# Norm panels started ahead of their sums, a reordered state-space tail and one table for log and exp, in a three-block transformer kernel

## The reference, cut to what matters

```python
def reference(x, mem, positions, ...):          # x is 256 x 2048, fp32
    x = first_block(...)     # even layer: gate conv + state-space mixer + memory attention
                             # odd layer: latent attention (MLA) + memory attention; then rms_norm
    return second_block(x, ...)   # retention layer, then squared_relu_mlp, final rmsnorm

def rmsnorm(x, g):           # stands before every projection
    return x * rsqrt(mean(x * x) + 1e-6) * g

# state-space output of one of 4 groups (512 columns), before w_out:
y = (y_diag + y_off + xs * d) * silu(z)
y = y * rsqrt(mean(y * y) + 1e-6) * ssd_norm_w
# retention:
x = x + (head_norm(o) * silu(g)) @ ret_w_out     # 8 heads, 512 columns each
x = x + square(relu(rmsnorm(x) @ w_up)) @ w_down
```

## Time and profile before

| what | us |
|---|---|
| median of 3 timed runs | 2857.05 (2854.23 to 2864.59) |
| span of the profiled execution | 2861.9 |
| TensorE busy | 2769.8 |
| VectorE busy | 1954.6 |
| ScalarE busy | 1405.5 |
| mean granted TensorE clock over the span | 0.986 |

### The profile page before, as it was taken

The page is one execution under the profiler, slowest core; times in us unless marked ns, Lnnn a source line. Parts: engine busy times, 40 slices in busy tenths (PEclk is TensorE's granted clock), DMA queues, the critical chain, the costliest instruction groups (busy, mean ns, idle before and its releaser), DMA issues.

```text
span 2861.9 us, 46279 instructions
## 1 busy us (share of the span) xinstructions
PE 2769.8 (97%) x15792; PEld 2412.3 (84%) x15792; DVE 1954.6 (68%) x3079; ACT 1405.5 (49%) x2199; POOL 35.4 (1%) x56
## 2 busy tenths in 40 slices
PE   6999999999999899999999999999999999999998
PEld 5888888888888788888888888888888888888887
DVE  5566567787767777777666655666667677576775
ACT  5544245555554555556555534555554444444444
POOL 0000000000000001000000000000000000000000
PEclk9999899999999999999999999999999999999999
DMA  5555354444664334465454455454445555555553
GB/s 230 193 190 191 119 193 151 154 147 149 199 226 152 112 128 159 150 194 182 169 179 172 172 176 182 177 179 171 152 166 188 191 189 191 191 191 190 187 188 110
DMA packets 76338, 495.57 MB, mean 173 GB/s; under 512 B 8544, under 2 KB 8672, under 8 KB 23792
## 3 DMA queue, kind: packets, MB, share of 16 engines
q1 hardware_dynamic: 73568, 478.18, 49.2%
q0 software_dynamic: 2000, 13.70, 1.3%
q10 hardware_dynamic: 704, 2.83, 0.3%
HBM read 486.29 MB, written 8.39 MB: 173 GB/s over the span
## 4 chain that ended last, share of the span: by engine, by line
PE 90%; DVE 4%; ACT 2%; issue 2%; DVEq 1%; DMA 0%; ACTq 0%; POOLq 0%
PE pj L1395 56%; PE pj L1398 28%; PE mx L1410 1%; ACT w_hi L403 1%; PE mx L1466 1%; DVE w_lo L727 1%; PE mx L1695 0%; PE mx L1636 0%; DVEq L930 0%; PE mx L1525 0%; PE mx L1637 0%; PE mx L1687 0%; PE mx L1702 0%; DMA xT<-in_mem 0%; PE mx L1513 0%
## 5 line engine op out<-in xcount | busy, mean ns | idle before, releaser
L1395 PE MATMUL pj<-hs,w_hi 128*128 128x512 f32 x4400 | 1562.2, 399 | 6.7 <-DVE xT L741 5.0
L727 DVE TENSOR_TENSOR w_lo<-raw,w_hi 128x1024 fp32r<-128x1024 f32 x1010 | 1137.0, 1130 | 480.6 <-ACT w_hi L403 463.0
L403 ACT ACTIVATE w_hi<-raw 128x1024 fp32r<-128x1024 f32 x1010 | 983.2, 979 | 672.7 <-PE pj L1395 669.2
L1398 PE MATMUL pj<-hs,w_lo 128*128 128x256 f32 x4400 | 1231.2, 280 | 0.0
L1395 PEld LDWEIGHTS pj<-hs,w_hi 128*128 128x128 f32 x4400 | 829.0, 188 | 198.9 <-DVE xT L741 5.3
L1395 PE MATMUL pj<-ys,w_hi 128*128 128x512 f32 x2560 | 906.3, 398 | 20.3 <-DVE ys L748 14.2
L1398 PEld LDWEIGHTS pj<-hs,w_lo 128*128 128x128 f32 x4400 | 833.6, 189 | 3.7 <-issue 2.9
L1398 PE MATMUL pj<-ys,w_lo 128*128 128x256 f32 x2560 | 720.5, 281 | 0.0
L1395 PEld LDWEIGHTS pj<-ys,w_hi 128*128 128x128 f32 x2560 | 483.8, 189 | 136.0 <-DVE ys L748 15.4
L1398 PEld LDWEIGHTS pj<-ys,w_lo 128*128 128x128 f32 x2560 | 487.8, 191 | 0.0
L408 ACT ACTIVATE half<-pj 128x256 f32<-128x256 f32 x491 | 186.9, 381 | 557.5 <-PE pj L1398 556.6
(11 more groups left out here) (262 smaller groups left out, 1356.4 us busy)
## 6 DMA issues: line engine op xcount, KB each, us to landing
raw<-in_w_up SPq DMA_DIRECT2D x64, 1024.0 KB, 4.8
raw<-in_w_down SPq DMA_DIRECT2D x64, 1024.0 KB, 4.8
raw<-in_w_ssd SPq DMA_DIRECT2D x48, 1024.0 KB, 4.8
raw<-in_w_ret_a SPq DMA_DIRECT2D x48, 1024.0 KB, 4.8
raw<-in_w_ret_b SPq DMA_DIRECT2D x48, 1024.0 KB, 4.8
raw<-in_w_out SPq DMA_DIRECT2D x64, 640.0 KB, 3.9
raw<-in_w_gate SPq DMA_DIRECT2D x32, 1024.0 KB, 4.8
raw<-in_w_mem SPq DMA_DIRECT2D x16, 1024.0 KB, 5.0
```

Of the source, the lines that this page charges most:

```text
L403: A(w_hi[:, s, 0:b - a, :], raw[:, c.slot(p, 4), a:b, :], ACT.Copy).then_inc(hi_ready, 1)
L727: TT(w_lo[:, s, 0:b - a, :], raw[:, c.slot(p, 4), a:b, :], w_hi[:, s, 0:b - a, :].bitcast(F32), ALU.subtract).then_inc(split_ready, 1)
L1395: ins = mm(pj[:, k], w_hi[:, s + h, u], m, start=opens and t == 0, stop=False)
L1398: ins = mm(pj[:, k, 0:T], w_lo[:, s + h, u], m[:, 0], start=False, stop=closes and t == len(moving) - 1)
```

## The change

The first panel behind a norm starts before the norm's sum: PE waits for all but the last tile of `hs`, does 11 tiles, then `square_sum` (now a `mid` call inside the panel), then the rest, the last tile waiting for its `hs`. DVE and ACT do the norm's steps inside the first panel's body, which is therefore written out ahead of the loop (`opening`). The latent and MLP norms lose the row sums, the last norm the column sum. Both norms behind out1 are found at once: the variance of the second is written as sum/D + eps * (sum of x * x) / D + eps * eps, so one Ln and one Exp over 516 columns serve both. The first two panels of a retention output run together: 12 tiles each, one wait, 4 tiles each. In the state-space tail y_off moves into panel 10, the gate into two steps, the squares are added on DVE so that one product inside panel 11 sums them; Newton comes before `y_mem`; ACT makes the hi parts of `ys`; the second half of a split comes after the scaling. `dte_ready` is waited for behind panel 1. `rsqrt` first loads one table that holds Ln and Exp. POOL's waits have new counts.

```diff
+LOG_EXP, EXP_TANH = "natural_log_exp_and_others", "exp_and_others"
 # POOL
-            pool.wait_ge(S["ssd_gated"], 4)
+            pool.wait_ge(S["ssd_gated"], 8)
             pool.dma_start(xflat[:, 0:2048], x_spill[:, 0:2048]).then_inc(S["x_loaded"], 16)
-            pool.wait_ge(S["y_ssd"], 4)
+            pool.wait_ge(S["y_ssd"], 16)
 # ACT
-            def rsqrt(k, v, y):
+            def rsqrt(k, v, y, weight=1):
+                nc.scalar.preload_act_table_set(LOG_EXP)
                 act.wait_ge(S["var_ready"], k)
                 A(y, v, ACT.Ln)
                 act.drain()
-                A(y, y, ACT.Exp, scale=-0.5).then_inc(S["rsqrt_ready"], 1)
+                A(y, y, ACT.Exp, scale=-0.5).then_inc(S["rsqrt_ready"], weight)
...
             def row_rsqrt(k, var, rsqrt_):
+                nc.scalar.preload_act_table_set(LOG_EXP)
...
                     if j == 11:
-                        act.wait_ge(S["ssd_gated"], i * 1 + 1)
-                        A(ssq, xs, ACT.Square).then_inc(S["ssd_squares"], 1)
+                        act.wait_ge(S["ssd_gated"], i * 2 + 1)
+                        A(ssq[:, 0:3], xs[:, 0:3], ACT.Square).then_inc(S["ssd_squares"], 1)
+                        act.wait_ge(S["ssd_gated"], i * 2 + 2)
+                        A(ssq[:, 3], xs[:, 3], ACT.Square).then_inc(S["ssd_squares"], 1)
                     split("ssd", i, j, 0)
...
+                    if j == 11:
+                        rsqrt(i * 1 + 1, em[0][:, 0:256], em[0][:, 256:512])
                     copy_half("ssd", i, j)
+                    if j == 11:
+                        nc.scalar.preload_act_table_set(EXP_TANH)
+                        act.wait_ge(evacuated, O(11, 1 + NB))
+                        A(th0, cv0, ACT.Tanh, scale=0.5).then_inc(S["mz_tanh"], 1)
                     split("ssd", i, j, 1)
-                act.wait_ge(evacuated, O(11, 1 + NB))
-                A(th0, cv0, ACT.Tanh, scale=0.5).then_inc(S["mz_tanh"], 1)
-                rsqrt(i * 1 + 1, em[0][:, 0:256], em[0][:, 256:512])
+                for n in range(4):
+                    act.wait_ge(S["ssd_y"], i * 4 + n + 1)
+                    A(ys[:, i * 4 + 4 + n, 0], xs[:, n], ACT.Copy).then_inc(S["y_ssd_hi"], 1)
...
+                        if opening and j == 0:
+                            rsqrt(NORM["b_ret"] + 1, nv2, ny2, 2)
 # DVE, state-space body
                     if j == 11:
+                        dve.drain()
+                        STT(out=xs[:, 3], in0=xs[:, 3], scalar=0.5, in1=sz[:, 3], op0=ALU.mult,
+                            op1=ALU.mult).then_inc(S["ssd_gated"], 1)
+                        dve.wait_ge(S["ssd_squares"], i * 2 + 1)
+                        TT(ssq[:, 0], ssq[:, 0], ssq[:, 1], ALU.add)
+                        dve.drain()
+                        TT(ssq[:, 0], ssq[:, 0], ssq[:, 2], ALU.add)
+                        dve.drain()
+                        dve.wait_ge(S["ssd_squares"], i * 2 + 2)
+                        TT(ssq[:, 0], ssq[:, 0], ssq[:, 3], ALU.add).then_inc(S["ssd_summed"], 1)
+                    split("ssd", i, j, 0)
+                    if j == 10:
                         dve.wait_ge(S["yoff_ready"], i * 1 + 1)
                         dve.wait_ge(S["eq_ready"], i * 1 + 1)
                         TT(eqx, mx[:, 0], eqx, ALU.mult)
                         dve.drain()
                         TT(xs[:, :, 128:256], xs[:, :, 128:256], eqx.rearrange("p (a q) -> p a q", a=4), ALU.add)
                         dve.drain()
-                        STT(out=xs_, in0=xs_, scalar=0.5, in1=sz_, op0=ALU.mult,
+                        STT(out=xs[:, 0:3], in0=xs[:, 0:3], scalar=0.5, in1=sz[:, 0:3], op0=ALU.mult,
                             op1=ALU.mult).then_inc(S["ssd_gated"], 1)
-                    split("ssd", i, j, 0)
+                    if j == 11:
+                        variance(i * 1 + 1, 5, 512, nrm[0])
                     evac("ssd", i, j, mq_s if j == 0 else cv0 if j == 11 else cp[(j - 1) % 2][:, 3:259])
-                    split("ssd", i, j, 1)
+                    if j < 11:
+                        split("ssd", i, j, 1)
+                dve.wait_ge(S["rsqrt_ready"], i * 1 + 1)
+                newton(*nrm)
                 dve.wait_ge(S["mz_tanh"], i * 1 + 1)
...
-                hi_lo((ys[:, bass.ds(i * 4 + 4, 4), 0], ys[:, bass.ds(i * 4 + 4, 4), 1]), xs).then_inc(S["y_ssd"], 1)
+                split("ssd", i, 11, 1)
+                for n in range(4):
+                    dve.wait_ge(S["y_ssd_hi"], i * 4 + n + 1)
+                    TT(ys[:, i * 4 + 4 + n, 1], xs[:, n], ys[:, i * 4 + 4 + n, 0].bitcast(F32),
+                       ALU.subtract).then_inc(S["y_ssd"], 1)
 # DVE, first panel of the retention stage (latent and up0 likewise, with variance() before evac)
+            def ret_variance():
+                dve.wait_ge(S["stat_ready"], NORM["b_ret"] + 1)
+                TS(nv2[:, 258:516], mx[:, 0, 0:258], 1.0 / D, EPS, ALU.mult, ALU.add)
+                TS(nt2[:, 0:258], mx[:, 0, 0:258], EPS / D, EPS * EPS, ALU.mult, ALU.add)
+                dve.drain()
+                STT(out=nv2[:, 0:258], in0=mx[:, 1, 0:258], scalar=1.0 / D, in1=nt2[:, 0:258], op0=ALU.mult,
+                    op1=ALU.add)
+                dve.drain().then_inc(S["var_ready"], 2)
...
+                        if opening and j == 0:
+                            ret_variance()
                         evac(name, i, j, dst, scale=rstd[:, 0:T] if j >= 8 else None)
                         split(name, i, j, 1)
+                        if opening and j == 0:
+                            ret_inverse()
+                            dve.drain()
+                            final_norm(0)
 # PE
-            def panel(name, i, j, pieces, before={}):
+            def panel(name, i, j, pieces, before={}, mid={}, late=()):
...
+                        if at + t in mid:
+                            mid[at + t]()
...
+            def two_panels(name, src, cut_, wait):
+                c, O = panels(name, 0), outputs(name, 0)
+                def some(j, a, b):
+                    s, k = 2 * c.slot(j, 2), O.slot(j, NB)
+                    for t in range(a, b):
+                        h, u = t // HALF, t % HALF
+                        if u == 0:
+                            pe.wait_ge(split_ready, c.half(j, h))
+                        ins = mm(pj[:, k], w_hi[:, s + h, u], src[:, t], start=t == 0, stop=False)
+                        if j == 0 and u == 0:
+                            ins.then_inc(half_started, 1)
+                        if j == 1 and t == cut_:
+                            ins.then_inc(half_started, 2)
+                        ins = mm(pj[:, k, 0:T], w_lo[:, s + h, u], src[:, t, 0], start=False, stop=t == 15)
+                    if b == 16:
+                        ins.then_inc(output_ready, 1)
+                for j in range(2):
+                    pe.wait_ge(evacuated, O(j, 1))
+                    some(j, 0, cut_)
+                pe.wait_ge(*wait)
+                for j in range(2):
+                    some(j, cut_, 16)
...
-                    whole("ssd", i, j, hs)
+                    whole("ssd", i, j, hs, mid={9: yoff} if j == 10 else {12: stat} if j == 11 else {})
+                    if j == 1:
+                        pe.wait_ge(S["dte_ready"], 1)
...
-            residual("out0", 2, ys, {3: (S["y_mem"], 4), 16: (S["y_ssd"], 4)})
-            square_sum()
-            pe.wait_ge(S["h_ready"], 16)
+            pe.wait_ge(S["y_ssd"], 12)
+            residual("out0", 2, ys, {3: (S["y_mem"], 4)} | {16 + n: (S["y_ssd"], 13 + n) for n in range(4)}, late=(3,))
...
+                        whole("latent", i, j, hs, {15: (S["h_ready"], 16)}, {11: lambda: square_sum(1)})
...
-                residual("ret_out" + ph[3:], 1, ys, {12: (S["y_ret"], first + 4)})
+                two_panels("ret_out" + ph[3:], ys, 12, (S["y_ret"], first + 4))
+                residual("ret_out" + ph[3:], 1, ys, {}, 2)
...
-            square_sum()
+            square_sum(4, rows=True, columns=False)
```

More of the change, by code:

```diff
@@ L584, in _, with latent_body @@
             residual("out0", 2)
[L585 to L594 removed]
+            def latent_body(i):
+                for j in range(4):
+                    split("latent", i, j, 0)
+                    if i == 0 and j == 0:
+                        rsqrt(NORM["b_latent"] + 1, nv, ny)
+                    copy_half("latent", i, j)
+                    split("latent", i, j, 1)
+            latent_body(0)
+            latent_body(1)
             act.wait_ge(S["angle_ready"], 1)
@@ L1387, in panel @@
                         pe.wait_ge(evacuated, O(o, 1))
-                    for t, m in enumerate(moving):
+                    order = [t for t in range(len(moving)) if t not in late] + list(late)
+                    for t in order:
+                        m = moving[t]
                         h = int(at + t >= half_)
@@ new lines, in square_sum @@
```

(10 more changed lines are left out.)

195 lines of the change are left out of this document (102 added, 93 removed).

## The result

In the first comparison the changed kernel had a median of 2829.61 us (2825.18 to 2830.99, 4 runs) against 2858.33 (2854.23 to 2864.59, 4 runs); the ratio is 0.9884, 95% interval 0.9859 to 0.9910. It is faster, by 1.2%. The profiled executions went from 2861.9 to 2827.5, 34.4 us less, where the prediction's sum was 45.3.

What follows compares the result with a forecast made beforehand. TensorE's panel stream, busy 97% of 2861.9 us, plus its stops and the slow clock behind long ones, was taken as the bound. Terms summed to 45.3 us: 2816.6 profiled, 2812 from the timed median 2857.05; range 2801 to 2830.

Steps and rivals of the forecast that it cites:

- the base: Median of the timed runs of the kernel before, 2857.05 us, from which the 45 us were taken to give 2812.
- The term for the MLP norm: up0's first panel starts before the norm's sum, leaving no stop; gain 7.3 us.
- Norms: First panels behind the latent, retention and MLP norms start before the sums; gains 7.0, 7.0 and 7.3 us.
- The covers: Spare time before a panel needs output 0 or 1: 2.3 us at latent's panel 2, 1.1 at retention's panel 3.
- Retention outputs: Both retention outputs, first two panels run together: no stop for L748, gain 7.5 us each, 15.0 in all.
- Tail: State-space tail: 3.4 us gained over three inner groups, 2.7 in the last group and out0's start.
- The table: One table for Ln and Exp: 1.3 us at the start; a 1.28 load leaves the chain to each retention output.
- Small ones: Exp wait before the state-space stage 0.5 us, one load at the start 1.3, column product at the end 1.1.
- (1): Rival: the state-space tail gives back its gain, four groups each stopping 2.5 us more; 2822 us, chance 0.12.
- (2): Rival: slow clock stays at five places, 2826 us, chance 0.05; or other slow stretches vanish, 2804, chance 0.07.
- (3): Rival: table loads stay despite the shared table, both retention outputs stop 0.6 us each; 2814.5 us, chance 0.05.
- (4): Rival: up to some 48 table loads delay ScalarE's weight splits, 61 us if all on the path; 2873 us, chance 0.03.

Runs made afterwards that it cites:

- The undo run: Changed kernel with the sums of the latent, retention and MLP norms put back ahead of the first panel; 2844.65 us.
- `a_no_table`: Changed kernel without the three hand-written table loads (the shared Ln and Exp table, and the Tanh one); 2828.38 us.
- `a_same`: Changed kernel run once more with no edit; 2830.12 us.
- `a_shift`: Changed kernel with four more instructions ahead of TensorE's first work, moving its later code by 256 bytes; 2825.90 us.
- `a_best`: `a_kick_up0` plus one product of 256 columns behind out1's first panel, with out1's first turn written out ahead of its loop; 2814.64 us.
- `a_kick_up0`: Changed kernel plus one product of two columns, result unused, behind up0's first panel; 2817.23 us, ratio 0.9840.

## Why the prediction was right, and what it missed

- **Time and range.** 2829.6 lies inside 2801 to 2830, 0.4 from its end; 2812 was 18 too low. Of these, 1.3 is the base, since 2857.05 became 2858.33 with a fourth run. The pace took 13.3 in the profiled pair of executions, the schedule gave 2.4 more than forecast, and the rest is the scatter of single runs: the profiled execution of before lay above its median. The gain in medians was 28.7, in the profiles 34.4. That the time fell inside the range is partly luck. The range was drawn for a weaker tail and for slow stretches, not for a pace of the pairs, and the same kernel measured again gave 2830.12, just outside.
- **The mis-sized term** is the unit of the first part: "a panel of 16 pairs takes 5.55 us at full clock, a pair 0.347". It was taken from two copies in ret_out_b, where the pace was fast, and used everywhere. The same trace had 353.3 in out0, latent, out1 and ret_out_a. Had I counted products in equal windows, I would have seen two levels at clock 1.00 and a risk of 13.5 on the slow side in the MLP alone. The term for the MLP norm, 7.3, took the sum's product inside the panel at its own length and gave no price to what it does to the pairs behind it; in every trace of the changed kernel that was 13.5.
- **Norms.** 6.9, 7.1 and 7.4 against 7.0, 7.0 and 7.3. Stops of 0.91, 1.26 and none against 0.9, 1.35 and none. The covers held: panel 3 of retention did not wait for output 1. The undo run confirms the split between idle time and clock.
- **Retention outputs.** 15.2 against 15.0; the second group of pairs starts without a wait. Without the pair of panels the stop is the 3.5 foreseen, without the table the 0.6.
- **Tail.** 4.3 and 3.1 against 3.4 and 2.7. The new stop in panel 11 is 0.93 to 0.94 in all four groups (forecast 1.0); out0 stops 1.80 at tile 3 (2.2), then 0.32 and 0.83 for the split (1.0).
- **The table** was priced in the places where I saw it, start and retention outputs. Its use for the tail's cover was left out: the text ahead of `a_no_table` still says that two loads stand there either way, but the one between Ln and Exp lies on VectorE's chain and the one for Tanh does not. It did not spoil the sum, since my tail was reckoned with the short chain anyway.
- **Small ones.** The start gained 0.5 in the first profile and 1.7 in that of `a_same` (a new stop ahead of the transposes was 0.89 and 0.50, and the first slow stretch of the clock 6.8 and 3.4 us long), the exp wait next to nothing, the last norm 2.2 (1.1).
- **Rivals.** (1) did not come: the tail gave nothing back. (2) did not come in the profile: all five slow stretches went. In `a_shift` and `a_best` 3.4 us at 0.50 stood behind out1 all the same. The argument against (2), the clock of 1.00 at the tail's stops, rested on one execution, and three of four traces with that tail read otherwise. (3) did not come. Of (4) the mechanism came and the price did not: ten loads stand ahead of a weight split, eight in the turns of the gate loop and two in memq, and eight more ahead of retention's Tanh (L706), so that there are 45 loads in all where the kernel before had 44. ScalarE had idle time there: the one wait of TensorE that names it after is at the memory queries (L1611), with 4.9 us in two stops as before. ScalarE's groups of loads (count, busy us and mean ns, idle before):
```profile
L414 ACT ACT_TABLE_LOAD x18 | 23.1, 1283 | 0.3
L405 ACT ACT_TABLE_LOAD x10 | 12.8, 1283 | 0.2
L706 ACT ACT_TABLE_LOAD x8 | 10.3, 1283 | 0.1
L587 ACT ACT_TABLE_LOAD x4 | 5.1, 1283 | 0.1
L431 ACT ACT_TABLE_LOAD x2 | 2.6, 1283 | 0.1
```
  The gain is in where the loads stand, not in how many there are. None of the four rivals was the pace.
- **The load's price.** ScalarE: Activation LUTs, What ACT_TABLE_LOAD costs, in the Trainium skill, has a drain of about 1380 ns behind a load. Behind the load at 1619.68 the Tanh starts at 1620.98, 1.30 later, so no trace here shows it. Table sets, the same page, says that one set holds both functions; the rows at 832.03 and 832.53 agree.

**Open.** What distinguishes the two paces inside TensorE, and which interruption leads to which. The order of products in the slow pace repeats every three pairs (starts 241, 120, 236, 113, 233, 117 ns apart), in the fast one every one or two (230, 117, or 231, 113, 232, 118). I tried no kernel that aims at this order. Whether the changed kernel ever runs its MLP fast is open too: in none of its 12 runs with unchanged products (2823.5 to 2832.1) did the time fall to that of the fast kernels (2818.3 at most).

## What to carry to other kernels

Where one engine streams like instructions for milliseconds, count them in equal windows of both kernels, not only stops and clock: 2% of pace over 2000 pairs hid over a quarter of this gain. A median cannot price a step that is smaller than such a state; match outputs one by one and read the step in its own stage. A cover of half a microsecond is worth writing down with all that it rests on: here the shared table carried it, and without it four places gave way.

## What was not expected of the hardware

- TensorE's pairs (512 and 256 columns) ran at 346.7 or 353.3 ns with the granted clock at 1.00. It changed nearly always behind other products or stops (at most seven changes in a trace came within a plain stream, most of them in mla), held for up to 2041 pairs, and could differ between executions of one program (gate at 353.3 in the changed kernel, at 346.7 in the same instructions of `a_kick_up0`).
- One product of 256 columns inside or just behind up0's first panel turned the pace over in ten traces of ten, six times to slow and four times to fast; one of two columns behind it did so in three of three (twice to fast, once to slow). Two of 256 columns in a row acted as one. Elsewhere a small product could leave the slow pace as it was.
- The granted clock stood at 0.50 for 3.4 us behind a stop of 1.26 to 1.35 us in three traces and stayed at 1.00 behind the same stop in seven.
